# The float32 projections of a two-layer hybrid decoder: their 512 columns walked in eight sweeps of every eighth 16-byte line, in place of four of every fourth

## Chip, cores and metric

The kernel runs on one core of a Trainium2 chip, in one launch. The metric is the device time of that launch in microseconds (us). The kernel before takes 2094.54 us, the median of three runs (2080.3, 2094.54 and 2095.16).

## The reference

256 tokens (SEQ) of width 2048 (D_MODEL) go through two residual layers. Layer 0 mixes tokens with stick-breaking attention (16 heads of 128), layer 1 with a chunked gMLP. Each is followed by a SwiGLU feed-forward of hidden width 5632, and a last RMSNorm ends it. All is float32.

```python
def swiglu_ffn(h, w_gate_up, w_down):
    gate, up = jnp.split(h @ w_gate_up, 2, axis=-1)
    return (jax.nn.silu(gate) * up) @ w_down

def reference(...):
    h = x
    for i in range(DEPTH):
        kind, j = i % N_MIXERS, i // N_MIXERS
        if kind == 0:
            h = h + stick_breaking_mixer(rmsnorm(h, sb_norm[j]), sb_w_qkv[j], sb_w_o[j])
        elif kind == 1:
            h = h + chunked_gmlp_mixer(rmsnorm(h, gm_norm[j]), gm_w_in[j], gm_v_norm[j],
                                       gm_w_s[j], gm_b_s[j], gm_w_o[j])
        h = h + swiglu_ffn(rmsnorm(h, ffn_norm[i]), ffn_w_gate_up[i], ffn_w_down[i])
    return rmsnorm(h, final_norm)
```

The work is in eight projections of the 256 tokens: 2048 by 6144 (query, key, value), 2048 by 2048 (attention output), 2048 by 11264 and 5632 by 2048 (feed-forward) in layer 0, and 2048 by 4096, 2048 by 2048, 2048 by 11264 and 5632 by 2048 in layer 1.

## The kernel before

Every projection is cut into pieces. A piece is a slab of KP = 2 contraction tiles of 128 rows by CH = 512 weight columns, 512 KB. There are 752 pieces, numbered through the whole program, and four engines work on them in a ring of RING = 4 slots:

- SyncE (SP) issues the load of a piece into `raw` (line 234), as soon as the piece four before it has been split.
- ScalarE (ACT) rounds it into `w_hi`, type float32r (`split`, line 359). VectorE (DVE) writes the rest, `raw - w_hi`, into `w_lo` (`split`, line 667). Both work LEAD = 3 pieces ahead of the matmuls.
- TensorE (PE) multiplies it (`piece`, lines 1096 and 1102). The activations are split in the same way, into `xT_hi` and `xT_lo` or `hid_hi` and `hid_lo`. For each contraction tile and each of the two blocks of 128 tokens it takes high by high and low by high (line 1096: eight matmuls a piece), and then high by low (line 1102: four). That makes 12 matmuls a piece. The stationary operand is a contiguous block of 128 by 128 activations, loaded anew for each matmul, and the moving operand is the 512 weight columns of one contraction tile.
- The result accumulates in PSUM in `acc`: two chunks of two token blocks, 512 float32 columns each. Semaphores (`hi_ready`, `lo_ready`, `used`) tie the engines together, and the order of the pieces is written out by hand.

Between the matmuls of the pieces, TensorE does the small products of the mixers: scores (line 1178), values (line 1198), the gMLP's position mixing (line 1327), and transposes (lines 1110, 1130 and 1186). The first two pieces go half by half (`early_products`, line 1144), and the last four of the last projection go token block by token block (lines 1368 to 1370). Together with these there are 752 times 12 = 9024 matmuls over weight columns.

All these matmuls read their moving operand and write `acc` through one helper, `swept`. It views 512 columns as c groups of SWEEPS runs of LINE float32 values, and puts the run's place in its group outermost:

```python
    LINE, SWEEPS = 4, 4
...
        def swept(columns):
            return columns.rearrange("p (c h e) -> p h c e", h=SWEEPS, e=LINE)
...
                            nc.tensor.matmul(swept(acc_at(chunk, r)), part[:, kt, rs], swept(w_hi[:, p % RING, k]),
                                             start=(kt == 0 and part is hi), stop=False)
```

A run is LINE = 4 float32 values, 16 bytes. With SWEEPS = 4 a matmul takes runs 0, 4, 8 up to 124 (a sweep of 32 runs, 64 bytes apart), then 1, 5, 9 and so on, then those from 2 and from 3. The output is walked in the same order, so each column's sum lands in its own place, and the readers of `acc` are not concerned. An unused tensor (`lead_in`) puts the region that holds `hid_hi` and `hid_lo` at the same address modulo 512 bytes as `w_hi`.

Of the kernel before, what the change touches and what calls it, by code (L numbers as in the profile page):

```python
# [5 lines left out]
def hybrid_trunk(nc, x, sb_norm, sb_w_qkv, sb_w_o, gm_norm, gm_w_in, gm_v_norm, gm_w_s, gm_b_s, gm_w_o,  # L6
# [36 lines left out]
    RING = 4  # L43
    LEAD = 3
    KP = 2
    LINE, SWEEPS = 4, 4
    PD = KD // KP
    PF = KF // KP
    assert PD % RING == 0 and 2 * PF % RING == 0
# [1354 lines left out]
```

How the kernel before makes its waits and increments, by code:

```python
        @block.sync  # L225
# [4 lines left out]
            def load(base, it, per, p, src, k0):  # L230
                if not (base == 0 and isinstance(it, int) and it == 0 and p < RING):
                    sp.wait_ge(lo_ready, base + it * per + p - RING + 1)
                sp.dma_start(raw[:, p % RING], src[:, k0:k0 + KP, :]).then_inc(raw_loaded[p % RING], 16)
# [56 lines left out]
                load(AT_GMI, 0, 2 * PD, t, w_in[:, :, c * CH + D:(c + 1) * CH + D], p * KP)  # L291
            for sec in range(2):
                with sp.Fori(2 * (1 - sec), ND) as c:
                    for p in range(PD):
                        load(AT_GMI + sec * ND * PD, c, PD, p, w_in[:, :, bass.ds(c * CH + (1 - sec) * D, CH)], p * KP)
            square(AT_GMO, gm_w_o[0])
            ffn(1)
            o = out.rearrange("(r p) n -> p r n", p=P)
            for done, n, r, cs in ((out_r0, 1, 0, slice(0, D)), (out_dve, 1, 1, slice(0, A // 3)),
                                   (out_dve, 2, 1, slice(A // 3, A)), (out_dve, 3, 1, slice(D - CH, D))):
                sp.wait_ge(done, n)
                sp.dma_start(o[:, r, cs], h[:, r, cs]).then_inc(stored, 16)
            sp.wait_ge(stored, 16 * 5)
# [2 lines left out]
        @block.gpsimd  # L306
# [2 lines left out]
                         (minus_half[:, :], -0.5), (left[:, ZW:ZW + 2], 1.0), (probT[:, :], 0.0)):  # L309
                nc.gpsimd.memset(t, v).then_inc(consts_filled, 1)
            pool.wait_ge(consts_filled, 7)
# [52 lines left out]
            def turned_gained(m, c, seen):  # L365
                act.wait_ge(n_turned[m], seen)
                for k in range(TC):
```

## Time and profile before

| | |
|---|---|
| median of three runs | 2094.54 us (2080.3 to 2095.16) |
| the profiled execution's own time | 2095.2 us |
| its span, first to last instruction | 2093.5 us |
| busy: PE, weight loads, DVE, ACT | 2083.9, 1725.1, 1430.5, 1012.2 us |
| matmuls in the trace | 9279, of them 9024 over weight columns |
| granted TensorE clock, mean | 0.999 of full speed |

PE is the matmul side of TensorE, PEld its weight loads (of the stationary operand), which lie beside the matmuls. The end of a matmul is modelled, so the distance from one start to the next tells more than its duration. A granted clock of 1.00 is 2.4 GHz.

### The profile page before, as it was taken

Reading aid. Unit: us, or ns where it says so; the run is one execution under the profiler, and the core shown is the slowest. Engines: PE = TensorE matmul, PEld = TensorE weight load, DVE = VectorE, ACT = ScalarE, POOL = GpSimd, SP = SyncE. Lnnn points to the kernel's source line nnn. Section 1 sums busy time; section 2 is a strip of 40 time slices with the busy share of each in tenths; the row PEclk is TensorE's granted clock in tenths of the full one; section 3 lists DMA queues with packets and bytes.
Section 4 is the critical chain, followed back from the end, with each engine's and each line's share of the span. In section 5 each row is a group of like instructions: output and inputs, shape, how many; then the busy total and the mean of one; then the engine's idle time right before and its main releaser. Section 6 shows DMA issues by size and latency. Waiting matters only on the chain.

```text
span 2093.5 us, 27155 instructions
## 1 busy us (share of the span) xinstructions
PE 2083.9 (100%) x9279; PEld 1725.1 (82%) x9279; DVE 1430.5 (68%) x1822; ACT 1012.2 (48%) x1285; POOL 16.5 (1%) x30
## 2 busy tenths in 40 slices
PE   9999999999999999999999999999999999999998
PEld 7888888888888888888888888888888888888887
DVE  7787787866666666665557887877666676664444
ACT  6677765444444444444445444554444444444443
POOL 1000000000000000000000000000000000000000
PEclk9999999999999999999999999999999999999999
DMA  8555655666666666555566665566666666655554
GB/s 272 181 189 154 192 178 174 205 193 192 192 191 196 191 193 194 195 191 193 194 196 207 187 203 186 190 186 203 193 190 194 193 194 192 191 195 197 191 191 150
DMA packets 207419, 402.47 MB, mean 192 GB/s; under 512 B 12336, under 2 KB 13056, under 8 KB 206976
## 3 DMA queue, kind: packets, MB, share of 16 engines
q1 hardware_dynamic: 206496, 398.11, 61.1%
q0 software_dynamic: 688, 3.18, 0.5%
q8 instruction: 36, 0.59, 0.1%
q10 hardware_dynamic: 176, 0.40, 0.1%
q14 instruction: 23, 0.19, 0.0%
HBM read 399.55 MB, written 2.10 MB: 192 GB/s over the span
## 4 chain that ended last, share of the span: by engine, by line
PE 94%; ACT 3%; DVE 2%; issue 1%; ACTq 0%; DVEq 0%; POOLq 0%; POOL 0%
PE acc L1096 61%; PE acc L1102 31%; ACT probT L437 1%; ACT w_hi L359 1%; DVE left L758 0%; DVE w_lo L667 0%; PE tp L1198 0%; PE tp L1327 0%; DVE prob_blk L772 0%; DVE prob L761 0%; PE tp L1178 0%; PE acc L1144 0%; PE acc L1137 0%; DVE prob L764 0%; PE tp L1110 0%
## 5 line engine op out<-in xcount | busy, mean ns | idle before, releaser
L667 DVE TENSOR_TENSOR w_lo<-raw,w_hi 128x1024 fp32r<-128x1024 f32 x750 | 915.8, 1224 | 582.5 <-ACT w_hi L359 578.9
L359 ACT ACTIVATE w_hi<-raw 128x1024 fp32r<-128x1024 f32 x750 | 792.5, 1060 | 919.1 <-PE acc L1102 914.1
L1096 PE MATMUL acc<-w_hi,xT 128*128 128x512 f32 x4080 | 1007.5, 387 | 0.0
L1096 PEld LDWEIGHTS acc<-w_hi,xT 128*128 128x128 f32 x4080 | 763.8, 188 | 157.2
L1102 PE MATMUL acc<-w_lo,xT 128*128 128x512 f32 x2040 | 543.7, 387 | 0.0
L1102 PEld LDWEIGHTS acc<-w_lo,xT 128*128 128x128 f32 x2040 | 382.5, 188 | 79.3
L1096 PE MATMUL acc<-w_hi,hid_hi 128*128 128x512 f32 x944 | 366.3, 388 | 0.0
L1096 PE MATMUL acc<-w_hi,hid_lo 128*128 128x512 f32 x944 | 365.1, 387 | 0.0
L1102 PE MATMUL acc<-w_lo,hid_hi 128*128 128x512 f32 x944 | 251.6, 387 | 0.0
L1102 PEld LDWEIGHTS acc<-w_lo,hid_hi 128*128 128x128 f32 x944 | 177.0, 188 | 36.9
L1096 PEld LDWEIGHTS acc<-w_hi,hid_hi 128*128 128x128 f32 x944 | 177.1, 188 | 36.7
L1096 PEld LDWEIGHTS acc<-w_hi,hid_lo 128*128 128x128 f32 x944 | 177.0, 188 | 36.5
L867 DVE STREAM_TRANSPOSE tp<-res 32x256 f32<-32x256 f32 x352 | 160.5, 456 | 7.9
L704 DVE STREAM_TRANSPOSE tp<-res 32x256 f32<-32x256 f32 x224 | 102.1, 456 | 4.5
L437 ACT ACTIVATE probT<-prob_blk 32x96 f32<-32x96 f32 x192 | 50.1, 261 | 29.7 <-DVE prob_blk L772 27.4
L546 ACT ACTIVATE gate<-acc,rstd 128x512 f32<-128x512 f32 x44 | 27.9, 685 | 33.3 <-PE acc L1102 33.2
L857 DVE SCALAR_TENSOR_TENSOR res<-acc,rstd,gate 128x512 f32<-128x512 f32 x44 | 31.0, 746 | 9.8 <-PE acc L1102 9.8
L746 DVE STREAM_TRANSPOSE k_t<-k_s 32x256 f32<-32x256 f32 x64 | 27.8, 435 | 1.2
L746 DVE STREAM_TRANSPOSE q_t<-q_s 32x256 f32<-32x256 f32 x64 | 27.8, 435 | 1.2
L876 DVE TENSOR_TENSOR hid_lo<-tp,hid_hi 128x1024 f32 (+1 forms) x22 | 26.8, 1218 | 0.0
L369 ACT ACTIVATE xT<-tp,cols 128x256 fp32r<-128x256 f32 (+1 forms) x48 | 19.0, 476 | 10.1 <-DVE tp L704 10.0
L758 DVE TENSOR_TENSOR_SCAN left<-keep,stop 128x384 f32<-128x384 f32 x16 | 15.3, 954 | 11.7 <-ACT take L421 11.7
(117 smaller groups left out, 430.2 us busy)
## 6 DMA issues: line engine op xcount, KB each, us to landing
raw<-in_ffn_w_gate_up SPq DMA_DIRECT2D x352, 512.0 KB, 4.5
raw<-in_ffn_w_down SPq DMA_DIRECT2D x176, 512.0 KB, 3.6
raw<-in_sb_w_qkv SPq DMA_DIRECT2D x95, 512.0 KB, 4.4
raw<-in_gm_w_in SPq DMA_DIRECT2D x64, 512.0 KB, 4.3
raw<-in_sb_w_o SPq DMA_DIRECT2D x32, 512.0 KB, 4.2
raw<-in_gm_w_o SPq DMA_DIRECT2D x32, 512.0 KB, 4.1
h<-in_x SPq DMA_DIRECT2D x3, 512.0 KB, 9.1
gain_bc<-in_gm_v_norm POOLq DMA_DIRECT2D x1, 1024.0 KB, 5.9
```

Of the source, the lines that this page charges most:

```text
L359: nc.scalar.activation(w_hi[:, p % RING], raw[:, p % RING], ACT.Copy).then_inc(hi_ready, 1)
L369: last = nc.scalar.activation(tile(xT_hi, c * TC + k), tp[0 if m or half(c) == 0 else 1][:, k * S:(k + 1) * S], ACT.Copy, scale=cols[:, ba ...
L437: last = nc.scalar.activation(dst[b * Q:(b + 1) * Q, ns, a], src[a * Q:(a + 1) * Q, ns, b], ACT.Copy)
L546: last = nc.scalar.activation(gate[:, r], acc_at(0, r), ACT.Silu, scale=rstd[:, 1 + 2 * layer, r:r + 1])
L667: nc.vector.tensor_tensor(w_lo[:, p % RING], raw[:, p % RING], w_hi[:, p % RING].bitcast(f32), ALU.subtract).then_inc(lo_ready, 1)
L704: last = nc.vector.transpose(tp[0][b * Q:(b + 1) * Q, :].rearrange("p (k r q t) -> p k r q t", k=TC, r=RT, q=4)[:, :, :, a], res[a * Q:(a ...
L746: last = nc.vector.transpose(dst[b * Q:(b + 1) * Q, :, :].rearrange("p k (r q t) -> p k r q t", r=RT, q=4)[:, :, :, a], src[a * Q:(a + 1) ...
L857: last = nc.vector.scalar_tensor_tensor(out=res[:, r], in0=acc_at(1, r), scalar=rstd[:, 1 + 2 * layer, r:r + 1], in1=gate[:, r], op0=ALU.m ...
L867: last = nc.vector.transpose(tp[1][b * Q:(b + 1) * Q, :].rearrange("p (k r q t) -> p k r q t", k=TC, r=RT, q=4)[:, :, :, a], res[a * Q:(a ...
L876: nc.vector.tensor_tensor(hid_lo[:, ks, :], tp[1][:, :].rearrange("p (k t) -> p k t", k=TC), hid_hi[:, ks, :].bitcast(f32), ALU.subtract). ...
L1096: nc.tensor.matmul(swept(acc_at(chunk, r)), part[:, kt, rs], swept(w_hi[:, p % RING, k]), start=(kt == 0 and part is hi), stop=False)
L1102: last = nc.tensor.matmul(swept(acc_at(chunk, r)), hi[:, kt, r * P:(r + 1) * P], swept(w_lo[:, p % RING, k]), start=False, stop=(kt == K - 1))
```

## The change

One number changes: SWEEPS goes from 4 to 8. A matmul takes its 512 columns in eight sweeps of 16 runs, 128 bytes apart, in place of four sweeps of 32 runs, 64 bytes apart. Run length, number of columns, stationary operand, and where each result lands stay as they are.

```diff
     RING = 4
     LEAD = 3
     KP = 2
-    LINE, SWEEPS = 4, 4
+    LINE, SWEEPS = 4, 8
     PD = KD // KP
     PF = KF // KP
```

On TensorE, at the start of the program (the first two pieces, then full pieces; `acc` is the accumulator, `w_hi` and `w_lo` the two parts of the weights, `xT` the activations), the two kernels stand against each other so:

```order
 L1137 MATMUL acc<-junk 128x512 x2
-L1144 MATMUL acc<-w_hi,xT 128x4x32x4 x4
-L1144 MATMUL acc<-w_lo,xT 128x4x32x4 x2
+L1144 MATMUL acc<-w_hi,xT 128x8x16x4 x4
+L1144 MATMUL acc<-w_lo,xT 128x8x16x4 x2
 L1130 MATMUL tp<-ident,h 128x128 x2
 L1130 MATMUL acc<-ident,h 128x128 x2
```

No instruction moves: the shape of the 9024 matmuls over weight columns changes (sweeps, runs in a sweep, values in a run), and on the other engines nothing does.

## Rows read from the trace of the kernel before

**Rows 1.** The page: span, busy time by engine, the granted clock in slices.
```profile
span 2093.5 us, 27155 instructions
PE 2083.9 (100%) x9279; PEld 1725.1 (82%) x9279; DVE 1430.5 (68%) x1822; ACT 1012.2 (48%) x1285; POOL 16.5 (1%) x30
PEclk9999999999999999999999999999999999999999
PE acc L1096 61%; PE acc L1102 31%; ACT probT L437 1%; ACT w_hi L359 1%; DVE left L758 0%; DVE w_lo L667 0%; PE tp L1198 0%; PE tp L1327 0%; DVE prob_blk L772 0%; DVE prob L761 0%; PE tp L1178 0%; PE acc L1144 0%; PE acc L1137 0%; DVE prob 
```

**Rows 2.** Windows of 200 us: busy us (instructions) by engine, granted clock, DMA share, GB/s.
```profile
400.00:600.00 200.00, 200.00 (x884) 165.46 (x883) 132.29 (x157) 89.87 (x93) 0.00 (x0) 1.00 0.66 194
...
1400.00:1600.00 200.00, 200.00 (x884) 165.49 (x883) 134.28 (x162) 88.43 (x89) 0.00 (x0) 1.00 0.65 193
...
1800.00:2000.00 200.00, 200.00 (x884) 165.50 (x883) 113.45 (x117) 83.48 (x86) 0.00 (x0) 1.00 0.60 193
```

**Rows 3.** Weights' waits: who waited, for whom, total us, times, longest.
```profile
ACT w_hi L359 <- PE acc L1102: 914.1, 577, 2.0
DVE w_lo L667 <- ACT w_hi L359: 578.9, 520, 3.9
```

**Rows 4.** Timeline of PE and PEld near the end: start us, duration us, then what.
```profile
2083.97 0.40 PE L1369 MATMUL acc<-w_lo,hid_hi 128*128 128x512 f32 x1
2083.98 0.19 PEld L1370 LDWEIGHTS acc<-w_hi,hid_lo 128*128 128x128 f32 x1
...
2084.88 0.38 PE L1370 MATMUL acc<-w_hi,hid_lo 128*128 128x512 f32 x1
2084.89 0.19 PEld L1368 LDWEIGHTS acc<-w_hi,hid_hi 128*128 128x128 f32 x1
2085.11 0.38 PE L1368 MATMUL acc<-w_hi,hid_hi 128*128 128x512 f32 x1
```

**Rows 5.** Timeline of PE in attention rounds, a stretch of close matmuls.
```profile
96.46 1.05 PE L1102 MATMUL acc<-w_lo,xT 128*128 128x512 f32 x4
97.36 1.95 PE L1096 MATMUL acc<-w_hi,xT 128*128 128x512 f32 x8
...
101.82 1.05 PE L1102 MATMUL acc<-w_lo,xT 128*128 128x512 f32 x4
```

**Rows 6.** Timeline of PE in attention rounds, a stretch of wider matmuls.
```profile
142.77 1.97 PE L1096 MATMUL acc<-w_hi,xT 128*128 128x512 f32 x8
...
161.81 0.38 PE L1178 MATMUL tp<-kT,qT 128*128 128x128 f32 x2
```

**Rows 7.** Lines: groups of full pieces, instructions, busy us, mean ns, idle before.
```profile
L1096 PE MATMUL acc<-w_hi,xT 128*128 128x512 f32 x4080 | 1007.5, 387 | 0.0
L1102 PE MATMUL acc<-w_lo,xT 128*128 128x512 f32 x2040 | 543.7, 387 | 0.0
L1102 PEld LDWEIGHTS acc<-w_lo,xT 128*128 128x128 f32 x2040 | 382.5, 188 | 79.3
L1102 PE MATMUL acc<-w_lo,hid_hi 128*128 128x512 f32 x944 | 251.6, 387 | 0.0
```

**Rows 8.** Timeline of the warm-up, contiguous bf16 columns: two weight loads in sequence.
```profile
2.36 0.15 PEld L1137 LDWEIGHTS acc<-junk 128*128 128x128 bf16 x1 [0.28 <-issue]
...
3.64 0.15 PEld L1137 LDWEIGHTS acc<-junk 128*128 128x128 bf16 x1 [0.28 <-issue]
```

## The prediction

> **What bounds the kernel now.** I read the page first. PE is busy for 2083.9 of 2093.5 us, DVE for 68% and ACT for 48%, and the granted clock is at its upper end in all slices but for rounding [rows 1]. The chain that ended last lies on the two lines of `piece`, 61% and 31% [rows 1]. The windows say the same more sharply: in each 200 us PE is busy for all 200.00 us at a granted clock of 1.00, which is 2.4 GHz, with 884 matmuls [rows 2]. The list of waits shows who is held: ACT waits 914.1 us for PE to free a ring slot, and DVE 578.9 us for ACT [rows 3]. The engines that prepare weights wait for TensorE, and none is waited for. So the time is the number of matmuls times the distance from one start to the next, and every ns of that distance counts 9024 times: 9.02 us per ns, 0.43% of the time.
>
> The distance: 200 us over 884 is 226.2 ns [rows 2]. The reader should see how even this is. DVE is busy for 132, 134 and 113 us in the three windows and DMA moves 194 and 193 GB/s, yet the count stays at 884. What the other engines do in memory does not move the distance.
>
> What could it be at best? The warm-up matmuls have 512 plain columns, and three of them pass between 2.36 and 3.64 us, 427 ns each [rows 8], which is one column per cycle at 1.2 GHz. One per cycle at 2.4 GHz would be 213.3 ns. So 226.2 carries about 12.9 ns above the pure stream, together 116 us of the whole time. That is all that an order of columns could win.
>
> The distance isn't one number either. At 96.46 us a row of 24 matmuls starts whose end is 101.82: 5.36 us over 24 is 223.3 ns [rows 5]. From 142.77 to 161.81 lie 84, and 19.04 over 84 is 226.7 ns [rows 6]. These are the same instructions on the same kinds of tiles. A row of matmuls settles into one of at least two rhythms and stays in it until a small product breaks the row. Inside a rhythm, starts differ: from 2084.88 to 2085.11 us is 0.23 us, and the four before it, from 2083.97, took 0.91, 227.5 each [rows 4]. Each weight load starts 0.01 us after the matmul before its own [rows 4] and takes 0.19, so the load of the next stationary block and the first part of the moving stream read SBUF together. The reader may take from this that the excess comes from two streams of TensorE itself meeting, or from the stream's own steps. The profile doesn't tell which.
>
> **The change, part by part.** No instruction is added, removed or moved. All 9024 matmuls over weight columns change the address pattern of the moving operand and of the output. Three things can carry a price.
>
> 1. Runs. Before and after a matmul reads 128 runs of 16 bytes and writes 128 such runs. Their number and length stay, so what hangs on leaving a run costs 0 more, and what it costs today is inside the 12.9 ns.
>
> 2. Turns between sweeps. There were 3 inside a matmul and one to the next matmul, and there will be 7 and one: 4 more. The trace shows no matmul over weight columns with another number of sweeps. Lower bound: 0 ns. Upper bound: the whole excess of today lies in the four turns, 12.9 / 4 = 3.2 ns each, then 4 more cost 12.9 ns, or 116 us. I take 0. The row nearest to this is the comparison of the two rhythms [rows 5, 6]: the same four turns cost 10.0 or 13.4 ns in all, so the excess isn't a fixed price per turn.
>
> 3. Distance of the runs, 128 bytes in place of 64, while the weight load walks a contiguous 512 bytes. If lines of memory are shared out by low address bits, a sweep now stays on fewer of them, or on the same few. A gain is bounded by 12.9 ns (116 us), a loss again by a doubling of the excess (116 us). The nearest rows for a small shift are again the two rhythms: 3.4 ns apart, 30 us over all matmuls. I take 0 for the middle: nothing in the trace says in which direction it goes.
>
> The weight loads keep form and length, 188 ns [rows 7], and 188 is less than 223, so they stay hidden. If the distance falls to 213 they would still be hidden. The cover for ACT and DVE is also wide: PE needs 12 times 226.2 = 2.71 us for a piece. In 200 us at 884 matmuls there are 73.7 pieces, and DVE is busy 132.29 / 73.7 = 1.79 us for each [rows 2], so even at 2.56 us a piece nothing is late next. DMA stands at a share of 0.66 at most [rows 2], and at a piece time 6% shorter it would be 0.70. Nothing eats a gain, and nothing hides a loss: since TensorE is alone on the path, whatever the distance does is seen in full.
>
> Sum: 0 + 0 + 0 on 2095.2 us, the profiled execution's own time (its span 2093.5 and 1.7 around it). It stands 0.7 above the median of 2094.54. I keep the median, 2094 us. One of the three runs was at 2080.3, 14 us lower. By the two rhythms that is what 14 / 0.0034 = 4100 matmuls in the closer rhythm would give, about one of the program's long uninterrupted rows. So the same kernel can differ by 14 us through this alone.
>
> A rule that speaks for no change is in the Trainium skill. The rows show a weight load beside each matmul, and 226.2 ns from start to start [rows 2, 4]. The page "TensorE: Matmul & The Clock Gate", in "Part 2: What happens when you issue a matmul", says that TensorE reads its weights and its moving operand over two independent ports, so that loading the next block takes nothing from the running stream. By that rule the collisions of point 3 don't exist, and the sum stays at 2094. The same page puts a warm stream of 512 columns at about 216 ns, and by that the excess of this kernel would be open, since the trace shows 10 ns more.
>
> A rule that speaks against the change is the one on PSUM. The row shows what a stream that jumps after every 16 bytes costs today, 226.2 ns [rows 2]. The page "PSUM — Partial Sum Buffer", in "Specifications (TRN2)", gives lines of 8 bytes and says that any pattern that isn't contiguous slows matmuls significantly. Both kernels write two such lines and jump, 128 times. Taken by the number of jumps the rule gives no change, and taken by their width it would favour the dear side of the bounds, up to 2210 us by the bounds above.
>
> **The rivals.**
>
> *Fewer meetings of load and stream (faster).* If the excess is the meeting of the contiguous weight load with the stream in the same part of memory, and the parts are told apart by the address within 128 bytes or more, a sweep with twice the step sits in half as many places and is met half as often. For it: the weight load starts with the matmul [rows 4], and the distance is blind to all other engines [rows 2]. Against it: with parts told apart within 64 bytes nothing changes. Price: half of 12.9 ns is 6.5, times 9024 = 58 us, so 2036.
>
> *Another rhythm (faster).* The new order leaves the causes alone but settles in the closer rhythm everywhere: 3.4 ns on some 8500 matmuls that are not in it already, 29 us, so 2065. For it: both rhythms occur in one run [rows 5, 6]. Against it: the long rows all stand at 884 in 200 us [rows 2].
>
> *The turns cost (slower).* The place is the turn from one sweep to the next, inside each matmul. If address generation or the accumulator's read and write has to settle at a turn, four more are paid. It decides against my forecast from 21 us on, 1% of the time: 21 / 9.02 / 4 = 0.6 ns a turn. The middle of its bounds is 1.6 ns, giving 58 us and 2152; the end is 2210. For it: an excess of 12.9 ns over four turns is there to be explained. Against it: the two rhythms.
>
> *The wider step hits fewer parts of memory (slower).* If a part of memory needs rest between two reads, a wider step comes back to the same one sooner. The excess grows by between nothing and its double, with 2152 in the middle.
>
> **How the numbers follow.** A measurement of this kernel can tell about 1% from no change. No change in the excess: 0.30, with a range of its own from 2074 to 2115. Fewer meetings: 0.20. Another rhythm: 0.14. Turns: 0.24. Wider step: 0.12. No change is the likeliest single case, hence 2094. Faster by over 1%: 0.20 + 0.14 = 0.34. Slower by over 1%: 0.24 + 0.12 = 0.36. Within: 0.30. The range takes in the two faster cases down to 2026, a little below 2036, and of the slower ones what lies below 2175, so that about a tenth is left out at either end.
>
> **What would show it.** In the profile after, the 200 us windows would again hold 880 to 888 matmuls if I am right. Some 910 would be fewer meetings (220 ns), 895 the other rhythm everywhere, and 860 or fewer one of the slower rivals. A distance that grows by the same amount in every matmul, whatever the rhythm, would speak for the turns, and an irregular one for meetings. DVE and ACT must keep their durations, ACT must still wait on PE for most of its idle time, and the granted clock must stay at 1.00. The prediction is wrong if the distance moves by more than 2.3 ns, or if PE is no longer busy throughout.

## The result

The changed kernel takes 2275.81 us, the median of four runs (2275.52 to 2276.18), against 2094.54 us. The ratio is 1.0871, with a 95% interval from 1.0845 to 1.0898: 8.7% slower, and outside the range of the prediction.

The page of the profile after, the lines that answer to [rows 1]:

```profile
span 2273.8 us, 27155 instructions
PE 2264.5 (100%) x9279; PEld 1771.2 (78%) x9279; DVE 1433.3 (63%) x1822; ACT 1016.7 (45%) x1285; POOL 13.8 (1%) x30
PEclk9999999999999999999999999999999999999999
```

The windows of 200 us after, answering to [rows 2] (busy us and instructions by engine, granted clock, DMA share, GB/s):

```profile
400.00:600.00 200.00, 200.00 (x812) 156.17 (x811) 126.83 (x158) 85.03 (x93) 0.73 (x1) 1.00 0.61 178
...
1800.00:2000.00 200.00, 200.00 (x813) 156.22 (x812) 122.12 (x144) 78.90 (x80) 0.00 (x0) 1.00 0.60 178
```

The waits after, answering to [rows 3]:

```profile
ACT w_hi L359 <- PE acc L1102: 1079.3, 590, 2.2
```

And the groups by line, answering to [rows 7]:

```profile
L1096 PE MATMUL acc<-w_hi,xT 128*128 128x512 f32 x4080 | 1093.1, 412 | 0.0
L1102 PEld LDWEIGHTS acc<-w_lo,xT 128*128 128x128 f32 x2040 | 392.9, 193 | 112.0
```

The reader should see one thing in these: the same instructions, the same engine busy without a gap, the same clock, and 812 matmuls in 200 us in place of 884. That is 246.3 ns for each in place of 226.2, and 20.1 ns times 9024 is 181 us. The two profiled spans are 180.3 us apart, so the distance explains all of it. (The count of a window takes in one or two matmuls that only reach into it. From the first start in the window to the last, the traces give 246.7 and 226.7 ns, which are the values that the expectations below use: 20.0 ns times 9024 is 180.5 us.) The modelled duration grew by 25 ns, 387 to 412. DVE and ACT do the same work in the same time and only wait longer: ACT waited 914.1 us for TensorE before, and now 1079.3.

The timeline of PE after, deep in the gate and up projection of layer 1, shows the new distance:

```profile
1700.77 2.14 PE L1096 MATMUL acc<-w_hi,xT 128*128 128x512 f32 x8
...
1703.72 0.66 PE L1096 MATMUL acc<-w_hi,xT 128*128 128x512 f32 x2
```

Twelve matmuls from 1700.77 to 1703.72 are 2.95 us, 246 ns each. Single distances can differ (in gate and up of layer 0 they take turns at 241, 243 and 256 ns), but their mean is 246.7 ns in all four feed-forward projections. The closer and the wider rhythm of before [rows 5, 6] are both gone from them.

### The profile page after: what moved, and what is told of

The parts are those of the page before. It is cut to its first block, busy times and chain, and to the rows that moved or that the text cites. A ratio compares the mean times of both kernels' runs of the same rounds, so it can differ in the third digit from the quotient of the medians.

```text
span 2273.8 us, 27155 instructions
## 1 busy us (share of the span) xinstructions
PE 2264.5 (100%) x9279; PEld 1771.2 (78%) x9279; DVE 1433.3 (63%) x1822; ACT 1016.7 (45%) x1285; POOL 13.8 (1%) x30
## 4 chain that ended last, share of the span: by engine, by line
PE 99%; issue 0%; DVE 0%; ACT 0%; POOLq 0%; POOL 0%; DVEq 0%; ACTq 0%
PE acc L1096 65%; PE acc L1102 32%; PE tp L1178 0%; PE tp L1198 0%; PE tp L1327 0%; PE acc L1144 0%; PE tp L1110 0%; PE acc L1137 0%; PE acc L1370 0%; PE acc L1369 0%; PE acc L1368 0%; PE tp L1186 0%; DVE h L1065 0%; ACT junk L635 0%; PE tp L1130 0%
## 5 line engine op out<-in xcount | busy, mean ns | idle before, releaser
L359 ACT ACTIVATE w_hi<-raw 128x1024 fp32r<-128x1024 f32 x750 | 794.1, 1062 | 1082.4 <-PE acc L1102 1079.3
L1096 PE MATMUL acc<-w_hi,xT 128*128 128x512 f32 x4080 | 1093.1, 412 | 0.0
L1096 PEld LDWEIGHTS acc<-w_hi,xT 128*128 128x128 f32 x4080 | 784.5, 193 | 216.5
L1102 PE MATMUL acc<-w_lo,xT 128*128 128x512 f32 x2040 | 586.4, 411 | 0.0
L1102 PEld LDWEIGHTS acc<-w_lo,xT 128*128 128x128 f32 x2040 | 392.9, 193 | 112.0
L1096 PE MATMUL acc<-w_hi,hid_hi 128*128 128x512 f32 x944 | 390.1, 413 | 0.0
L1096 PE MATMUL acc<-w_hi,hid_lo 128*128 128x512 f32 x944 | 387.7, 411 | 0.0
L1102 PE MATMUL acc<-w_lo,hid_hi 128*128 128x512 f32 x944 | 271.3, 411 | 0.0
L1102 PEld LDWEIGHTS acc<-w_lo,hid_hi 128*128 128x128 f32 x944 | 181.8, 193 | 51.9
L1096 PEld LDWEIGHTS acc<-w_hi,hid_lo 128*128 128x128 f32 x944 | 181.9, 193 | 50.3
L552 ACT ACTIVATE hid_hi<-tp 128x1024 f32 (+1 forms) x22 | 22.6, 1025 | 0.0
```

Source lines behind the costliest of these rows:

```text
L359: nc.scalar.activation(w_hi[:, p % RING], raw[:, p % RING], ACT.Copy).then_inc(hi_ready, 1)
L552: nc.scalar.activation(hid_hi[:, bass.ds(i * TC, TC), :], tp[1][:, :].rearrange("p (k t) -> p k t", k=TC), ACT.Copy).then_inc(f_hi[layer], 1)
L1102: last = nc.tensor.matmul(swept(acc_at(chunk, r)), hi[:, kt, r * P:(r + 1) * P], swept(w_lo[:, p % RING, k]), start=False, stop=(kt == K - 1))
```

## The experiments

In most of these kernels each stage has its own order of columns, so that one run gives five readings. A reading is the length of a window inside the stage over the number of matmuls in it. It is a little low, since the count takes in one or two matmuls at the edge: against the mean from start to start by 0.2 to 0.7 ns in windows of 200 and 400 us (by 1.0 at runs of 8 bytes), and by 1 to 2 ns in windows of 60 to 80 us. Where that matters, the value from start to start is given too. The stages and the instruction counts are those of before. The diffs are against the kernel before and show only what differs in meaning (the order is handed to `swept` as an argument, and lines left out are marked by `...`). In them, `(line, sweeps)` is a pair of values for run and sweeps, first of the moving operand, then of the output.

**Number of sweeps.**

```diff
-    LINE, SWEEPS = 4, 4
+    ROW = ((4, 4), (4, 4))
...
+    ORDERS = ((AT_UP[0], ((4, 1), (4, 1))),
+              (AT_DOWN[0], ((4, 2), (4, 2))),
+              (AT_GMI, ((4, 16), (4, 16))),
+              (AT_UP[1], ((4, 32), (4, 32))),
+              (AT_DOWN[1], ((4, 8), (4, 8))))
```

> Every stage has its own number of sweeps of 16-byte runs, in moving operand and output: 4 in the query, key, value and output projections of layer 0, 1 (plain columns) in its gate and up projection, 2 in its down projection, 16 in the two gMLP projections, 32 in gate and up of layer 1, 8 in its down projection. The known distances from one matmul's start to the next are 226.7 ns at 4 and 246.7 at 8. Turns (5.0 ns for each turn more, as 20.0 over 4 turns): 1 gives 211.7 to 216, 2 gives 217, 16 gives 287, 32 gives 367. Step between runs (the wider, the sooner the same part of memory comes back): 1 and 2 at or below 226.7, 16 and 32 well above 246.7, but not along a line: at some step all runs fall on one part and it stays level. Both agree that 8 is 246.7 in the last stage. Meetings with the weight load: 1 is dearer than 4, since load and stream walk the same lines in step.

Windows of PE alone in this kernel, for 1, 2, 32 and 8 sweeps, and then for 16 (from the gMLP's output projection):

```profile
400.00:800.00 400.00, 400.00 (x1766) 1.00 0.65 193
880.00:1080.00 200.00, 200.00 (x867) 1.00 0.57 190
...
1500.00:1900.00 400.00, 400.00 (x1494) 1.00 0.57 163
2000.00:2200.00 200.00, 200.00 (x812) 1.00 0.53 177
```

```profile
1350.00:1420.00 70.00, 70.00 (x255) 1.00 0.49 158
```

Plain columns take 226.5 ns, 2 sweeps 230.7, 16 sweeps 274.5 (276.1 from start to start), 32 sweeps 267.7 and 8 sweeps 246.3, as in the changed kernel. A price per turn would have given 367 at 32. It isn't one: 32 is cheaper than 16. And plain columns stand where 4 sweeps do, so that a row of the four sweeps gains nothing.

**Which side.**

```diff
+    ORDERS = ((AT_UP[0], ((4, 8), (4, 4))),
+              (AT_DOWN[0], ((4, 4), (4, 8))),
+              (AT_GMI, ((4, 8), (4, 1))),
+              (AT_UP[1], ((4, 1), (4, 8))),
+              (AT_DOWN[1], ((4, 4), (4, 1))))
```

> Moving operand and output walk the columns in different orders, so that sums land in other columns in these stages: gate and up of layer 0 reads in 8 sweeps and writes in 4, its down projection reads in 4 and writes in 8, the gMLP projections read in 8 and write plainly, gate and up of layer 1 reads plainly and writes in 8, its down projection reads in 4 and writes plainly. If the 20.0 ns sit in the read of the weights from SBUF: 246.7 where 8 is read, 226.7 where 4 is read, whatever is written. If they sit in the accumulator: 246.7 where 8 is written, 226.7 where 4 is written. If both have a share, the two mixed stages lie between.

Windows of PE: read 8 and write 4; read 4 and write 8; read plainly and write 8; read 4 and write plainly.

```profile
450.00:850.00 400.00, 400.00 (x1623) 1.00 0.61 177
910.00:1110.00 200.00, 200.00 (x885) 1.00 0.58 193
...
1450.00:1850.00 400.00, 400.00 (x1766) 1.00 0.65 193
1930.00:2130.00 200.00, 200.00 (x897) 1.00 0.59 196
```

246.5, 226.0, 226.5 and 223.0 ns. The distance follows what is read, and the accumulator can be walked in any of these orders, all of 16-byte runs, for nothing. The whole price of the change is in the read of the weights from SBUF. The Trainium skill ("PSUM — Partial Sum Buffer", "Specifications (TRN2)") says that any pattern that isn't contiguous slows matmuls significantly; with eight sweeps or four on the output beside plain ones, these rows show no such slowing.

**Turns or step.** With 16-byte runs and full coverage, the number of sweeps fixes the step. Here the moving operand reads 128 runs from its ring slot in an order of its own (turns, step in bytes, runs in a sweep); the output is written plainly. By the access pattern, the two widest orders (4 turns at 128 bytes, 8 at 256) read each of their 128 runs once, over the slot's 4096 bytes. The others read some runs again: 8 turns at 64 bytes take 68 different ones, 8 at 16 bytes 23, and 16 at 64 bytes 44.

```diff
+    ORDERS = ((AT_UP[0], ((4, 128, 32), (4, 1))),
+              (AT_DOWN[0], ((8, 64, 16), (4, 1))),
+              (AT_GMI, ((8, 16, 16), (4, 1))),
+              (AT_UP[1], ((16, 64, 8), (4, 1))),
+              (AT_DOWN[1], ((8, 256, 16), (4, 1))))
...
+                return bass.AP(tensor=columns.tensor, offset=offset,
+                               ap=[[columns.ap[0][0], P], [4, turns], [step // 4, runs], [1, 4]])
```

> Number of sweeps and step taken apart with 16-byte runs, 128 of them in each matmul, by letting the moving operand read other runs of the same ring slot (some twice, others never, so the products are others; the output is written plainly). Gate and up of layer 0: 4 sweeps of 32 runs, 128 bytes apart. Down of layer 0: 8 sweeps of 16 runs, 64 bytes apart. gMLP projections: 8 sweeps of 16 runs, 16 bytes apart. Gate and up of layer 1: 16 sweeps of 8 runs, 64 bytes apart. Down of layer 1: 8 sweeps of 16 runs, 256 bytes apart. Turns: 226.7 in the first, 246.7 in the second, third and fifth, 277 in the fourth. Step: 246.7 in the first, 226.7 in the second and fourth, 226.7 in the third, 277 in the fifth. A sweep's last and next first run meeting (a turn goes back by a whole sweep and lands on a part just read) would give values between.

Windows of PE in the order of the diff:

```profile
400.00:800.00 400.00, 400.00 (x1580) 1.00 0.59 172
920.00:1120.00 200.00, 200.00 (x872) 1.00 0.57 191
1360.00:1430.00 70.00, 70.00 (x302) 1.00 0.57 188
1450.00:1850.00 400.00, 400.00 (x1820) 1.00 0.68 199
1950.00:2150.00 200.00, 200.00 (x706) 1.00 0.46 155
```

| sweeps | step, bytes | ns |
|---|---|---|
| 4 | 128 | 253.2 |
| 8 | 64 | 229.4 |
| 8 | 16 | 231.8 |
| 16 | 64 | 219.8 |
| 8 | 256 | 283.3 |

Four sweeps at a step of 128 bytes are as dear as the change and more. Sixteen at 64 bytes are the cheapest of all, where a price per turn wanted 277, though they read some runs again. The two orders that read each run once need no such reserve, and they can be held against the orders of the first experiment, since how the output is written costs nothing. At 128 bytes four sweeps take 253.2 ns and eight 246.3; at 256 bytes eight take 283.3 and sixteen 274.5. More turns at one step are cheaper there, by 7 to 9 ns, and not dearer. (At 16 bytes, eight sweeps take 231.8 ns, or 233.3 from start to start, and one 226.5.) So it is the step, and turns bring no price that grows with their number. This settles the main question: the change is slow because its 16-byte runs are 128 bytes apart.

**Length of a run.** A longer run makes fewer steps of the same width.

```diff
+    ORDERS = ((AT_UP[0], ((8, 4), (8, 4))),
+              (AT_DOWN[0], ((2, 8), (2, 8))),
+              (AT_GMI, ((8, 2), (8, 2))),
+              (AT_UP[1], ((16, 2), (16, 2))),
+              (AT_DOWN[1], ((16, 4), (16, 4))))
```

> Step and number of sweeps taken apart by the length of a run: gate and up of layer 0 has 4 sweeps of 32-byte runs, 128 bytes apart; its down projection 8 sweeps of 8-byte runs, 64 bytes apart; the gMLP projections 2 sweeps of 32-byte runs, 64 bytes apart; gate and up of layer 1 has 2 sweeps of 64-byte runs, 128 bytes apart; its down projection 4 sweeps of 64-byte runs, 256 bytes apart. Turns: the distance follows the number of sweeps, 4 gives 226.7, 8 gives 246.7, 2 gives some 217, whatever the step. Step: 128 bytes gives 246.7 with 4 and with 2 sweeps, 64 bytes gives 226.7 with 8 and with 2. If jumps inside a sweep are what costs, the longer runs are all cheaper, and the 8-byte runs are the dearest.

Windows of PE: 32-byte runs 128 apart; 8-byte runs 64 apart; 64-byte runs 128 apart; 64-byte runs 256 apart; and, in the gMLP's output projection, 32-byte runs 64 apart.

```profile
400.00:800.00 400.00, 400.00 (x1736) 1.00 0.65 190
900.00:1300.00 400.00, 400.00 (x930) 1.00 0.31 101
...
1700.00:2100.00 400.00, 400.00 (x1668) 1.00 0.62 182
2110.00:2310.00 200.00, 200.00 (x837) 1.00 0.55 184
```

```profile
1530.00:1590.00 60.00, 60.00 (x260) 1.00 0.57 187
```

230.4, 430.1, 239.8, 238.9 and 230.8 ns (232.4 from start to start). The first says that 128 bytes between runs of 32 cost 4 ns over before, not 20: it is the step between runs of 16 bytes that is dear. The second is the strongest effect of the study. Runs of 8 bytes take 430 ns, close to twice plain columns, and 512 columns in runs of two are 256 runs in place of 128. The Trainium skill ("SBUF — State Buffer", "Specifications (TRN2)") gives lines of 16 bytes, a penalty for each change of line, and full bandwidth from two hits in a line on. The trace agrees with a price for more changes of line, but these runs have two hits in each line and are far from full speed. It can't be laid to SBUF alone, since the accumulator is written in 8-byte runs in this stage too, and the free orders of the experiment before had runs of 16. Neither my turns nor my step predicted these readings: the step wanted 246.7 ns for the first, and in the third and fourth a 64-byte run makes plain steps of 16 bytes and a jump after every fourth. What held is that a longer run is cheaper at the same step (246.3 ns with 16-byte runs at 128 bytes, 274.5 at 256), though not at 64 (226.2), and that 8-byte runs are the dearest.

**Load against stream.** The weight load of the next matmul lies beside each stream. First, `w_hi` is moved by 64 bytes against `xT`, and `hid` (`hid_hi` and `hid_lo`) by 32 against `w_hi`.

```diff
+        pad = sb("pad", [P, 16])
         raw = sb("raw", [P, RING, KP, CH])
...
-        lead_in = sb("lead_in", [P, (nc.lookup_mloc(w_hi).addr - used_up_to) % CH // 4])
+        lead_in = sb("lead_in", [P, (nc.lookup_mloc(w_hi).addr - used_up_to) % CH // 4 + 8])
```

> w_hi and w_lo move 64 bytes against the activations xT (an unused tensor between them), and hid_hi and hid_lo sit 32 bytes further against w_hi. 8 sweeps in gate and up, down and both gMLP projections, 4 elsewhere. Meetings of the weight load with the stream in the same part of SBUF: the distance changes with the shift, away from 246.7 at 8 sweeps and from 226.7 at 4, by 3 ns or more in at least one stage. Turns, or a step that meets its own lines: 246.7 and 226.7 stay in every stage to 1 ns.

Windows of PE: 8 sweeps on `xT`, 8 on `hid`, 4 on `xT`, 4 on `hid`.

```profile
400.00:800.00 400.00, 400.00 (x1669) 1.00 0.63 182
900.00:1100.00 200.00, 200.00 (x835) 1.00 0.55 183
1440.00:1840.00 400.00, 400.00 (x1793) 1.00 0.66 196
1900.00:2100.00 200.00, 200.00 (x884) 1.00 0.58 193
```

Eight sweeps fall to 239.7 and 239.5 ns. A second kernel with 8 sweeps in the first two stages moves everything by 64 bytes, activations and weights alike:

```diff
+        pad = sb("pad", [P, 16])
         h = sb("h", [P, RT, D])
```

> Everything in SBUF moves up by 64 bytes, the activations with the weights, so that load and stream stand to each other as before and only their absolute place changes. 8 sweeps in gate and up and down of layer 0, plain columns in the gMLP projections, 4 sweeps elsewhere. If the place of the moving operand alone sets the distance: 240.0 at 8 sweeps, as in the kernel where w_hi was moved by 64 bytes. If the place of load against stream does: 246.7, 226.7 and 226.7 as without any shift.

```profile
400.00:800.00 400.00, 400.00 (x1623) 1.00 0.61 177
920.00:1120.00 200.00, 200.00 (x813) 1.00 0.54 178
...
1450.00:1850.00 400.00, 400.00 (x1793) 1.00 0.66 196
1920.00:2120.00 200.00, 200.00 (x898) 1.00 0.60 197
```

246.5 and 246.0 ns at 8 sweeps: moving both by 64 bytes doesn't matter, but moving the load against the stream does. The two stages with 4 sweeps, which stood at 226.2 before, run here at 223.1 and 222.7, the closer rhythm of [rows 5] for a whole projection, though nothing in them is shifted against anything. So a row can settle in either.

Two further kernels have other shifts:

> w_hi and w_lo are moved by 128 bytes against xT (stages on xT: 8 sweeps in gate and up of layer 0, plain in the gMLP input projection, 4 sweeps in query, key, value and in gate and up of layer 1), and hid sits 256 bytes further against w_hi (8 sweeps in down of layer 0, plain in the gMLP output projection, 4 in down of layer 1 and in the attention output projection). Meetings, with parts told apart by address bits below 128 bytes: back to 246.7, 226.7 and 226.7 as without a shift, where 64 and 32 bytes gave 240.0 at 8 sweeps. Parts told apart by higher bits: other distances again in at least one stage. The stream alone: no shift does anything, which the 240.0 already speaks against.

Windows of PE with `w_hi` moved by 128 bytes against `xT`, 8 sweeps and 4:

```profile
400.00:800.00 400.00, 400.00 (x1638) 1.00 0.61 180
...
1450.00:1850.00 400.00, 400.00 (x1669) 1.00 0.62 183
```

> The same stages with w_hi moved by 32 bytes against xT, and hid 96 bytes further against w_hi. Meetings: 8 sweeps are again away from 246.7, since 32 bytes gave 240.0 on hid, and plain columns and 4 sweeps move by some ns to either side of 226.7 in at least one stage, with 220 within reach where load and stream keep out of each other's way. The stream alone: 246.7, 226.7 and 226.7 everywhere.

| shift of load against stream, bytes | 8 sweeps, ns | 4 sweeps, ns |
|---|---|---|
| 0 | 246.3 | 226.2, in other kernels 223.0 |
| 32 on `xT` | 247.7 | 219.8 |
| 32 on `hid` | 239.5 | 226.2 |
| 64 | 239.7 | 223.1 |
| 96 | 246.0 | 225.7 |
| 128 | 244.2 | 239.7 |
| 256 | 246.3 | 223.0 |

These are 400 us over 1615, 1820, 1638 and 1669 matmuls and 200 us over 813, 886, 812 and 897 in the same kind of windows. A shift moves 8 sweeps by 7 ns at most and 4 sweeps by up to 20, in no order that I can name, and the same 32 bytes give different distances on two tensors whose weights also stand elsewhere. With `w_hi` moved by 128 bytes against `xT`, 4 sweeps are nearly as dear as 8 (239.7 against 244.2). So the 20 ns of the change hold for the place that load and stream have in these two kernels; at the shifts tried, 8 sweeps cost between 4 and 28 ns more than 4. They were never brought down to 4 at the same shift. And since 4 sweeps stand at 223.0 or at 226.2 with no shift at all, a difference of 3 ns can't be laid to one.

**Is the step's price paid in the stream alone?** Three kernels change the weight load itself. In the first the stationary operand is one activation column taken 128 times, in the second every second token, in 8, 4, 1, 16 and 32 sweeps by stage.

```diff
+            return part[:, kt, r * P:r * P + 1].to_broadcast([P, P])
```

```diff
+            return part[:, kt, r:2 * P:2]
```

> From layer 0's gate and up projection on, the stationary operand of the full pieces is one activation column taken 128 times, so that a weight load has the same 128 columns but reads one 16-byte line in place of 32; the products are others. 8 sweeps in gate and up of layer 0, 4 in its down projection, plain columns in the gMLP projections, 16 sweeps in gate and up of layer 1, 32 in its down projection. Meetings of load and stream: with nearly nothing to meet, the distance falls to some 216 ns in every stage, whatever the number of sweeps. The stream alone (its turns or its own step is what costs): 246.7 at 8, 226.7 at 4 and at 1, 277 at 16 and 268 at 32 stay.

> The same stages and sweeps, but the stationary operand takes every second token of the 256, so that a weight load still has 128 columns and touches 64 lines in place of 32, two values from each; the tokens land in other rows. Meetings: the part above 213.3 grows by up to a factor of two in each stage, 8 sweeps from 33 to as much as 67 ns (280), 4 sweeps and plain columns from 13 to 27 (240). The stream alone: no change, 246.7, 226.7, 226.7, 277 and 268.

Windows of PE with the one column, 8, 4 and 16 sweeps, and then with every second token, 8 sweeps.

```profile
400.00:800.00 400.00, 400.00 (x1624) 1.00 0.61 177
910.00:1110.00 200.00, 200.00 (x905) 1.00 0.59 198
...
1450.00:1850.00 400.00, 400.00 (x1439) 1.00 0.55 157
```

```profile
400.00:800.00 400.00, 400.00 (x1635) 1.00 0.62 179
```

246.3 ns at 8 sweeps, as if nothing had been done; 221.0 at 4 and 278.0 at 16. With every second token, 8 sweeps took 400 / 1635 = 244.6, 4 sweeps 200 / 895 = 223.5, and 16 sweeps 400 / 1431 = 279.5. The 32 sweeps stay at 266.0 and 268.1 (752 and 746 matmuls in 200 us). Meetings wanted 216 and up to 280 at 8 sweeps. Whether a repeated column is read once or 128 times the trace doesn't show, so the third kernel shortens the load: both down projections take 32 tokens in place of 128 and leave out three quarters of their sums.

```diff
+            return part[:, kt, r * P:r * P + (Q if base in AT_DOWN else P)]
```

> In both down projections the stationary operand is 32 tokens in place of 128, so that a weight load has 32 columns and 8 lines, and three quarters of the sums are left out. Order of the columns as in the run before: 4 sweeps, 8, plain, 16. A cost that arises beside the weight load shrinks with the load: the part above 213.3 falls to a quarter or so, 8 sweeps from 33 to some 8 ns (222), 4 sweeps and plain to 217, 16 sweeps to 229. A cost of the stream alone: 246.7 and 277 stay.

Windows of PE at 4, 8, 1 and 16 sweeps:

```profile
880.00:960.00 80.00, 80.00 (x361) 1.00 0.59 196
1000.00:1080.00 80.00, 80.00 (x326) 1.00 0.54 179
1860.00:1940.00 80.00, 80.00 (x347) 1.00 0.57 190
1990.00:2070.00 80.00, 80.00 (x291) 1.00 0.47 159
```

221.6, 245.4, 230.5 and 274.9 ns, from start to start 222.9, 246.7, 231.7 and 277.1. A load of 32 columns takes 110 ns in this trace, where one of 128 takes 188. Eight and sixteen sweeps don't notice that three quarters of the load's columns are gone. Four sweeps gain 4 ns, and plain columns lose 5.

The last two take the load of the next matmul away from beside the stream. In `one_by_one` each matmul of the down projections waits for the one before it:

```diff
+                            after_last(n)
+                            done(nc.tensor.matmul(swept(acc_at(chunk, r), written), part[:, kt, rs],
```

> In both down projections every matmul waits for the one before it, so that no weight load lies beside a stream: 4 sweeps in the first half of the layer 0 stage, 8 in its second half, plain columns in the first half of the layer 1 stage, 16 in its second. Everything is far slower there, some 500 to 700 ns a matmul, and only the differences count. The stream alone: the second halves are dearer than the first, 8 sweeps by 20 ns over 4, and 16 by 50 over plain. Meetings of load and stream: no difference beyond 2 ns.

Windows of PE inside the halves with 4, 16 and 8 sweeps:

```profile
1050.00:1200.00 150.00, 137.36 (x175) 0.50 0.15 49
2900.00:3050.00 150.00, 137.36 (x175) 0.50 0.16 52
```

```profile
1250.00:1400.00 150.00, 137.48 (x174) 0.50 0.16 52
```

It answered another question than the one asked. In both projections the granted clock fell from 1.00 to 0.50, which is 1.2 GHz, after TensorE had been idle between the matmuls (busy for 174.52 of 200 us in the window from 2500 to 2700 us, still at 1.00). At 0.50, 150 us hold 175 matmuls at 4 sweeps, 174 at 8 and 175 at 16: 863 ns from start to start at each. Between matmuls that wait for each other at half the clock the step costs nothing, where at the full one 4, 8 and 16 sweeps lie 20 and 28 ns apart. Only four sweeps and plain columns ran alone at the full clock, both at some 560 ns. So the run was inconclusive for 8 and 16 there, and the next one keeps the clock up: only the sixth of twelve matmuls is alone.

```diff
+                    if serial and n in (5, 6):
+                        pe.wait_ge(alone[layer], (it * per + p) * 2 + n - 4)
```

> In both down projections the sixth matmul of each piece starts only when the fifth is done, and the seventh only when the sixth is, so that the sixth streams with no weight load beside it while the piece as a whole keeps the clock up. 4 sweeps in the first half of the layer 0 stage, 8 in its second, plain columns in the first half of the layer 1 stage, 16 in its second. The distance from the sixth start to the seventh is the lone stream with its way out and the next load, 560 ns by the first such run at 4 sweeps and with plain columns. The step costs in the stream itself: 580 at 8 sweeps and 610 at 16. It costs only where a weight load lies beside the stream: 560 in all four.

Timeline of PE in this kernel (whose line 1126 is line 1096 of before), the lone matmul and the one after it, at 4 sweeps, 8, plain, and 16 (the clock stayed at its upper level):

```profile
951.07 0.49 PE L1126 MATMUL acc<-w_hi,hid_lo 128*128 128x512 f32 x1
951.61 0.49 PE L1126 MATMUL acc<-w_hi,hid_hi 128*128 128x512 f32 x1
```

```profile
1101.25 0.51 PE L1126 MATMUL acc<-w_hi,hid_lo 128*128 128x512 f32 x1
1101.81 0.52 PE L1126 MATMUL acc<-w_hi,hid_hi 128*128 128x512 f32 x1
```

```profile
2000.94 0.50 PE L1126 MATMUL acc<-w_hi,hid_lo 128*128 128x512 f32 x1
2001.50 0.50 PE L1126 MATMUL acc<-w_hi,hid_hi 128*128 128x512 f32 x1
```

```profile
2149.50 0.54 PE L1126 MATMUL acc<-w_hi,hid_lo 128*128 128x512 f32 x1
2150.09 0.54 PE L1126 MATMUL acc<-w_hi,hid_hi 128*128 128x512 f32 x1
```

0.54, 0.56, 0.56 and 0.59 us, and nearly the same in every piece of these stages: 547, 564, 560 and 599 ns on the mean. The trace puts the lone matmul's own load at its start; the load of the next one begins only after its end. Over four sweeps, eight cost 17 ns more and sixteen 52, much as in a row (20 and 50). Sixteen sweeps are clearly dearer alone, whatever they are held against. For eight the run doesn't decide: plain columns alone take 560 ns, only 4 less, and in `one_by_one` the same sixth matmul at four sweeps took 550 to 560 ns at the full clock, not 547. So that the price of eight sweeps arises in the stream's own read rests on the shortened load, which left it at 246.7 ns; the lone stream shows it for sixteen.

**Better than before?** `plain` uses one sweep everywhere, and `closer_32` keeps four sweeps and shifts load against stream by 32 bytes.

```diff
-    LINE, SWEEPS = 4, 4
+    ROW = ((4, 1), (4, 1))
```

```diff
+        pad = sb("pad", [P, 8])
         raw = sb("raw", [P, RING, KP, CH])
...
-        lead_in = sb("lead_in", [P, (nc.lookup_mloc(w_hi).addr - used_up_to) % CH // 4])
+        lead_in = sb("lead_in", [P, (nc.lookup_mloc(w_hi).addr - used_up_to) % CH // 4 + 8])
```

> All 9024 matmuls take their columns and write the accumulator in plain order, one sweep. By the stage that had it, 226.7 ns, the same as 4 sweeps: 2094, and no difference from the kernel before beyond 0.7%. If the turns or jumps of the 4 sweeps cost anything, it is faster, and if the sweeps are what keeps load and stream apart, slower.

> 4 sweeps everywhere as in the kernel before, with w_hi moved by 32 bytes against xT and hid another 32 bytes against w_hi. In gate and up of layer 1 that shift of w_hi gave 220.0 ns. If the shift of load against stream is what counts, that holds in every stage on xT, some 6100 matmuls: 6.7 ns each is 41 us, so 2054, and 2035 if the stages on hid follow. If it is a rhythm that a stretch falls into by chance: anything between 2035 and 2095.

`plain` took 2096.86 us (2096.32 to 2096.99, 10 runs), a ratio of 1.0036 with an interval from 1.0013 to 1.0059. So the four sweeps of before are worth 0.4%, and 0.6% at most. `closer_32` took 2072.87 us (2072.34 to 2074.66, 4 runs), 0.9909 with an interval from 0.9874 to 0.9944: 0.9% faster than the kernel before, whose fastest of seven runs beside it took 2081.89. It came neither to 2054 nor to 2035. Its windows of PE in gate and up of layer 0 and of layer 1:

```profile
400.00:800.00 400.00, 400.00 (x1777) 1.00 0.65 194
...
1400.00:1800.00 400.00, 400.00 (x1820) 1.00 0.67 199
```

225.1 and 219.8 ns. Both down projections stay at 226.2, with 884 matmuls in 200 us. Most of the gain sits in the second gate and up: 2112 matmuls at 6.7 ns less are 14 of 22 us. The first runs the same code at the same addresses and stays 5 ns wider, so the shift doesn't give a fixed price. That it gives a choice of rhythm is the reading that fits; what picks the rhythm wasn't tested.

## Why the prediction was wrong

The forecast was no change, 2094 us in 2026 to 2175. The time went to 2276.

- *What bounds the kernel.* Right. TensorE is busy throughout before and after, and 20.1 ns times 9024 gives the 181 us. The floor of 213.3 ns under the 12.9 was less sure than it looks: the clock records of the trace begin only at 6.9 us, behind the warm-up matmuls that it was read from, and no run came closer than 219.8 ns.
- *Point 1, the runs: 0.* Their number and length stayed, but the step between 16-byte runs was what cost. I had priced leaving a run as the same whatever the distance jumped.
- *Point 2, the turns: 0 taken.* Right in that four more turns cost nothing: at a step of 128 bytes eight sweeps took 7 ns less than four, and at 256 bytes sixteen 9 ns less than eight.
- *Point 3, the distance of the runs: 0 taken, bounded at 12.9 ns either way.* This is the step that failed. The term was put at 0, with 12.9 ns (116 us) as its upper end, and it measured 20.1 ns (181 us). The bound was made by doubling the excess of today, and nothing in the trace supports that doubling as an end: a pattern that the trace has never shown has no upper bound from one that it has. The half-priced middle of both slower rivals, 6.5 ns, was three times too small for the same reason. With 0.36 for slower I had the sign as likely as any, and still let the range end at 2175.
- *Which rival came true.* The wider step. It had 0.12, the smallest chance. The turns had 0.24, and the experiments give them nothing. What came true is that the step costs; the reason given for it, parts of memory that need rest, isn't shown, and 512 bytes being cheaper than 256 doesn't follow from it as it stands. Its price was outside its own bounds, too.
- *Fewer meetings, 0.20.* Load and stream do touch each other: a shift between them moves 8 sweeps by 7 ns and 4 sweeps by more. But a load of one column repeated, or of a quarter of the columns, leaves 8 sweeps at 246.7, and the change made the kernel slower. It is a second effect, and at a shift of 128 bytes nearly as large as the first.
- *Another rhythm, 0.14.* It exists, and a whole projection can sit in it (223.1 in the kernel moved by 64 bytes). The change didn't bring it: the new order has one mean distance of its own. The 4100 matmuls that were to explain the run at 2080.3 us are more than the longest uninterrupted row, which has 3168, and no trace of such a run was taken. That rhythms make the difference between runs stays likely and not shown.
- *The argument from evenness.* I took it that the distance ignores the other engines. That held: in the traces before and after, every 84 matmuls of the feed-forward stages take the same mean within 0.1 ns, whatever DVE, ACT and DMA do meanwhile.
- *The rule of two read ports.* The page "TensorE: Matmul & The Clock Gate" of the Trainium skill ("Part 2: What happens when you issue a matmul") says that a load takes nothing from the stream. The shifts show that it isn't wholly so here: 246.3 against 239.7 ns at 8 sweeps, and 226.2 against 239.7 at 4. By the shortened load it is so for 8 and 16 sweeps, which stay where they were.

Open is why plain columns differ from four sweeps alone but not in a row, what makes a row of matmuls choose its rhythm, and how the memory behind the steps is laid out. The steps 16, 32, 64, 128, 256 and 512 bytes gave 226.5, 230.7, 226.2, 246.3, 274.5 and 267.7 ns, which rise and fall too irregularly for a simple rule of shared parts. Open is also whether runs of 8 bytes are dear in the read, in the accumulator or in both.

## What to carry to other kernels

Where TensorE is busy without a gap, the distance between the starts of its matmuls is the kernel, and the address pattern of the moving operand belongs to it: read runs of at least 16 bytes in order or at most 64 bytes apart, and measure any other order, and any new placement of the stationary operand against the moving one, before using it (one shift brought the 64-byte step to 239.7 ns). Several orders can be tried in one run by giving each stage its own and counting matmuls in windows. A bound for a pattern that no row shows must not be a multiple of today's excess.

## What the runs showed of the hardware

- Step between 16-byte runs of the moving operand (float32r) at 2.4 GHz, from start to start: up to 64 bytes 220 to 233 ns for 512 columns in an unshifted kernel, 128 bytes 247 to 253, 256 bytes 276 to 284.
- Runs of 8 bytes, 64 apart, read and written so: 431 ns.
- The order in which the accumulator is written costs nothing in the orders tried (plain, four and eight sweeps of 16-byte runs).
- At 1.2 GHz, 4, 8 and 16 sweeps cost the same, 863 ns alone. At 2.4 GHz in a row, they take 226.7, 246.7 and 276.1 ns from start to start.
- A row of the same matmuls can run at 219.8, 223 or 226.2 ns, and holds it for hundreds of microseconds. The place of the weight load against the stream bears on it but doesn't settle it: two stages with the same code and addresses ran at 225.1 and 219.8.
- Over 13 runs the kernel before stood at 2081.5 to 2082.8 us five times and at 2093.4 to 2095.5 eight times, with nothing between.
